# Last gated layer's output product in seven block products on half tiles, with weight sums made in the convolution layer and kept in DRAM

## The reference: what is computed

```python
def mixer_a(h, w_in, b_in, vn_g, vn_b, w_s, b_s, w_out):
    z = gelu(h @ w_in + b_in)                 # (S, 6144)
    u, v = split(z, 2)                        # (S, 3072) each
    v = layernorm(v, vn_g, vn_b)              # then cut into chunks of 128 positions, 8 groups
    gate = einsum('gts,csgd->ctgd', tril(w_s), v) + b_s
    return (u * gate) @ w_out                 # (S, 3072) @ (3072, 1024)
...
def mixer_c(h, w_in, w_dw, b_dw, ln_g, ln_b, w_out):
    a, g = split(h @ w_in, 2)                 # (S, 1024) each
    y = a * sigmoid(g)
    y = causal_depthwise_conv31(y, w_dw) + b_dw
    return silu(layernorm(y, ln_g, ln_b)) @ w_out
...
def channel_mlp(h, w1, w2):
    return square(relu(h @ w1)) @ w2          # 1024 -> 4096 -> 1024
```

## Time and profile before

| | us |
|---|---|
| three runs | 3079.35, 3292.37, 3439.02 (median 3292.37) |
| the profiled execution, its own time | 3079.77 |
| its span on the slowest core (core 3) | 3078.2 |
| around the span | 1.6 |
| spans of the 8 cores | 3070.2 to 3078.2 |

### The profile page before, as it was taken

The page is one execution under the profiler, slowest core; times in us unless marked ns, Lnnn a source line. Parts: engine busy times, 40 slices in busy tenths (PEclk is TensorE's granted clock), DMA queues, the critical chain, the costliest instruction groups (busy, mean ns, idle before and its releaser), DMA issues.

```text
span 3078.2 us, 47408 instructions; the slowest of 8 cores (3070.2 to 3078.2 us)
## 1 busy us (share of the span) xinstructions
PE 3019.1 (98%) x15290; PEld 1439.1 (47%) x15290; DVE 2267.6 (74%) x3775; ACT 1317.5 (43%) x2293; POOL 738.5 (24%) x896
## 2 busy tenths in 40 slices
PE   8999999999999999999999999999999999999998
PEld 3444444444444444444576444444444444444444
DVE  7945767678779987877458788877855757577886
ACT  4312433434655354455534634553322333433554
POOL 1111233101414320132551421212212141201221
PEclk9999999999999999999999999999999999999999
DMA  9699997777867367686422477768897988776674
GB/s 167 109 152 165 165 160 126 164 158 156 165 154 130 62 154 158 150 204 150 104 47 77 100 174 172 166 149 165 140 162 131 160 135 143 155 163 142 153 188 114
DMA packets 137585, 445.45 MB, mean 145 GB/s; under 512 B 12032, under 2 KB 15232, under 8 KB 137344
## 3 DMA queue, kind: packets, MB, share of 16 engines
q0 software_dynamic: 102304, 347.38, 64.4%
q1 hardware_dynamic: 35040, 95.04, 8.7%
HBM read 646.07 MB, written 78.64 MB: 235 GB/s over the span
## 4 chain that ended last, share of the span: by engine, by line
PE 93%; DMA 2%; DVE 2%; issue 1%; ACT 1%; POOL 0%; SPq 0%; DVEq 0%; ACTq 0%; POOLq 0%
PE bank L164 93%; DVE xT L164 1%; DMA xT<-x 1%; DMA x_spill<-xT 1%; DMA ring<-b_w_out 0%; DMA ring<-m_w 0%; DVE m_tv L164 0%; DVE bank L164 0%; DVE hT1v L164 0%; DMA ring<-a_w_in 0%; ACT ring L164 0%; ACT sq L164 0%; ACT rs L164 0%; POOL sacc L164 0%; POOL a_smv L164 0%
## 5 line engine op out<-in xcount | busy, mean ns | idle before, releaser
L164 DVE TENSOR_TENSOR xT<-bank,xT 128x512 f32<-128x512 f32 (+2 forms) x972 | 707.3, 745 | 290.5 <-PE bank L164 270.6
L164 PE MATMUL bank<-m_tv,ring 128*128 128x512 bf16 (+2 forms) x3724 | 814.7, 372 | 11.2 <-DVE xT L164 9.3
L164 PEld LDWEIGHTS bank<-m_tv,ring 128*128 128x128 bf16 x3724 | 358.4, 98 | 434.3 <-issue 24.8
L164 ACT ACTIVATE bank<-bank 128x512 f32<-128x512 f32 x496 | 289.4, 587 | 416.1 <-PE bank L164 340.1
L164 POOL DMA_DIRECT2D ring<-m_w x256 | 137.6, 537 | 1242.4 <-PE bank L164 1189.8
L164 ACT ACTIVATE m_tv<-bank 128x512 bf16<-128x512 f32 x511 | 302.2, 598 | 46.7 <-DVE bank L164 11.2
L164 DVE TENSOR_TENSOR m_tv<-m_tv,m_tv 128x512 bf16<-128x512 bf16 x494 | 221.5, 479 | 97.7 <-ACT m_tv L164 94.9
L164 POOL TENSOR_TENSOR sacc<-sacc,sq 128x512 f32<-128x512 f32 (+1 forms) x162 | 212.0, 1309 | 95.4 <-ACT sq L164 64.0
L164 DVE TENSOR_TENSOR ring<-ring 128x512 bf16<-128x512 bf16 (+1 forms) x384 | 199.9, 537 | 26.7 <-DMA ring<-m_w 18.4
L164 ACT ACTIVATE sq<-xT 128x512 f32<-128x512 f32 (+1 forms) x252 | 152.8, 620 | 144.1 <-POOL sacc L164 91.3
L164 PE MATMUL bank<-m_hv,ring 128*128 128x512 bf16 x704 | 174.6, 379 | 2.2 <-issue 0.3
(11 more groups left out here) (242 smaller groups left out, 4186.5 us busy)
## 6 DMA issues: line engine op xcount, KB each, us to landing
ring<-a_w_in POOLq DMA_DIRECT2D x88, 1024.0 KB, 15.2
ring<-m_w POOLq DMA_DIRECT2D x132, 512.0 KB, 7.1
m_pre<-ring SPq DMA_DIRECT2D x124, 512.0 KB, 6.3
ring<-m_pre POOLq DMA_DIRECT2D x124, 512.0 KB, 7.3
ring<-a_w_out POOLq DMA_DIRECT2D x64, 768.0 KB, 8.5
ring<-m_w POOLq DMA_DIRECT2D x124, 384.0 KB, 6.4
xT<-x SPq DMA_DIRECT2D x16, 512.0 KB, 12.8
ring<-b_w_in POOLq DMA_DIRECT2D x8, 1024.0 KB, 18.7
```

The costliest lines, as they stand in the source:

```text
L164: return lambda e: getattr(e, _method)(*[_r(a) for a in args], **{k: _r(v) for k, v in kwargs.items()})
```

## The change

The output product of layer 3's mixer A (`WO`) is replaced by `WO7`, and only there (`self.seven`); layer 0 keeps `WO`.

- A tile's 512 positions are cut in two halves of 256, the 1024 outputs in two halves, and the 3072 inner channels, in three groups of 8 blocks (`b`), each in two halves of 4 blocks. For each of 4 output pairs `d` there are seven products, each of 3 x 4 = 12 matmuls of 256 columns.
- The sums of activations (`usums`, four DVE operations of 1024 elements for each of the three groups) are made as soon as a group's 8 blocks are through `SP`; three of the four results lie in `v`, the fourth replaces a part of `uT`.
- The sums of weights are made once, in the convolution layer: 12 units, each a load of 2048 elements (1 MB of f32), three DVE operations (`wsums`) and a store of 3584 bf16 elements for each partition to `a_wp` in DRAM, in rows of 512 elements. They use two ring slots lent for that (`lend_slot`, `lent`), so that layer 2 has three, and four from its fourth stage on.
- Each product's weights are then one piece of 128 x 1536 bf16 in DRAM, loaded by SP, two pieces to a slot, 28 pieces for each tile.
- DVE adds a product of 256 columns to `xT` 6 times for each `d`, and one of 512 (a result that goes to two places).
- The norm of the next tile becomes steps within `WO7`; the first V load of tiles 1 to 3 is cut into two halves.

```diff
+    def lend_slot():
+        lent.append(take_slot() + (sc.dma_key(f"unit{len(lent)}"), sc.dma_key(f"unit_out{len(lent)}")))
+
+    def next_unit(after):
+        if makes:
+            d, b = makes.pop(0)
+            lent.append(lent.pop(0))
+            t, r, _, key, out_key = lent[-1]
+            v, vr = views(t, r)
+            sc.op("pool", I("dma_start", out=t[:, 0:2048], in_=dram["a_w_out7"][d * 3 + b], max_dma_last_dim=8192), wr=[vr[k] for k in QUADS[:4]],
+                  cost=0.75, dma=key, nbytes=512 * 2048, after=after, tag="unit", lat=LOAD_LAT)
+            wsums(t, v, vr)
+            sc.op("sp", I("dma_start", out=a_wp[d, :, :, b * 512:(b + 1) * 512].rearrange("k p c -> p k c"),
+                          in_=t[:, 512:4096].rearrange("p (k c) -> p k c", k=7)), rd=[vr[k] for k in QUADS[1:]], wr=[wp_r[d][b]],
...
+            def usums(b):
...
+                for o, x, y in (("S1", "A21", "A22"), ("m2", "A11", "S1"), ("m3", "A21", "A11"), ("n4", "A12", "m2")):
+                    comb(A[(o, b)][0], A[(o, b)][1], *A[(x, b)], *A[(y, b)], ALU.subtract, 1024)
+
+            def WO7(tt, steps):
...
+                def piece(d, wk):
+                    j = place[1] % 2
+                    place[1] += 1
+                    if j == 0:
+                        t, r, key = take_slot()
+                        place[0] = t, r.split(2), key
+                    t, rs, key = place[0]
+                    o = sc.op("sp", I("dma_start", out=t[:, j * 1536:(j + 1) * 1536], in_=a_wp[d, QUADS.index(wk) - 1]),
+                              rd=wp_r[d], wr=[rs[j]], cost=0.06, dma=pc_key[slot_of(t)][j], nbytes=256 * 1536, tag="load")
...
+                for d in range(4):
+                    a, f, e, g = Bank(), Bank(), Bank(), Bank()
+                    prod(a, "A11", "W11", True)
+                    add(a, 0, 0)
+                    prod(f, "A12", "W21", True)
+                    add(f, 0, 0)
+                    prod(e, "m3", "n3", True)
+                    add(e, 1, 1)
+                    prod(a, "m2", "n2", False)
+                    add(a, 0, 1)
+                    prod(g, "n4", "W22", True)
+                    add(g, 1, 0)
+                    prod(e, "A22", "T4", False)
+                    add(e, 0, 1)
+                    prod(a, "S1", "T1", False)
+                    add(a, 1, 2)
+                    if d == 2:
+                        for q in steps:
+                            run_all(q)
...
+            UNIT_AT = (2, 6, 10, 14), (2, 6, 10), (2,), (2, 10), ()
...
+                if i == 3 and lent:
+                    lent.pop(0)
...
                     for vp in range(6):
-                        V(tt, vp, load_v(vp))
+                        V(tt, vp, load_v(vp, 2 if self.seven and tt and vp == 0 else 1))
```

More of the change, by code:

```diff
@@ L549, in take_slot @@
     def take_slot():
-        i = ring_n[0] % NSLOT
-        ring_n[0] += 1
-        return ring[i]
+        while True:
+            i = ring_n[0] % NSLOT
+            ring_n[0] += 1
+            if ring[i][0] not in [x[0] for x in lent]:
+                return ring[i]
     def load_w(name, idx, blk, view, after=(), parts=1):
@@ L1315, in body @@
                     load_x(2, (3,), after=last_sp)
-                    mid = lambda after: self.norm(2, after=after, mode="dve")
+                    mid = lambda after: run_all(self.norm_steps(2, after=after, mode="dve"))
                 elif tt + 1 < NT:
-                    self.norm(tt + 1, after=[late_u[0]])
+                    steps = [self.norm_steps(tt + 1, after=[late_u[0]])]
                 else:
-                    for e in early:
-                        run_all(e)
-                WO(tt, mid)
+                    steps = early
+                if self.seven:
+                    WO7(tt, steps)
+                else:
+                    for q in steps:
+                        run_all(q)
+                    WO(tt, mid)
     class MixB:
@@ L1840, in body @@
             for b in norm_bufs:
[L1841 removed]
+                b.r |= lent_r.used()
+            assert not makes
+            lent.clear()
     for j in range(16):
```

103 lines of the change are left out of this document (76 added, 27 removed).

## The result

The changed kernel takes 3090.6 us (median of 12 executions), the kernel before 3079.5 (12, on the same chip): ratio 1.0033, 95% interval 1.0023 to 1.0043. The time lies inside the range of the forecast, on the other side of the kernel before.

The account below looks back on a forecast made before the run. PE was taken to bound the kernel, 93% of the chain. The terms -17.1 + 4 + 3 + 2 + 3 + 1 = -4.1 on 3079.8 us gave 3075.7, stated as 3076 us, range 3060 to 3100.

Parts of the forecast that it names:

- The products' term: Layer 3's output product: 1344 matmuls of 256 columns for 768 of 512 gain 17.1 us, bounds 13 and 21.
- The rival that it doesn't halve: Layer 3's product: a 256-column matmul does not halve; at 125 ns nothing is gained, 3093 us; chance 0.03.
- that of weight loads that don't overlap: Layer 3's product: 576 more weight loads of 98 ns add 56 us, giving 3132 us; chance 0.02.
- I count no steady wait: Pieces in layer 3's product: loading lags 2.2 us a tile, less than 10 us of supply ahead, so no cost.
- The +4 for the start: Start of each layer 3 product: PE waits for pieces or activation sums, 1 us a tile, +4, from 0 to 12.
- The second rival: Layer 3's product: the SP queue, waiting for slots in turn, starves PE of pieces; 3100 us, slower; chance 0.2.
- V's late start: V of tiles 1 to 3: its first load just arrives, 1 us of wait each, +3, from 0 to 15.
- DVE full in tile 3: Tile 3's product: DVE busy 36.4 of 37.5 us, its delays reach PE through the banks; +2, from 0 to 6.
- The convolution layer and the next MLP: Making weight sums costs the convolution layer +3 (-3 to +12); loads delayed by lent slots and unit stores +1 (0 to 4).
- The stats chain: Convolution layer's stats chain: the last two units' sums before `c_z` cost +3, load and store waits +1.
- the nothing for ten units: Convolution layer stages: ten of twelve units cost nothing, as DVE and DMA have room.
- The third rival: Convolution layer: DVE stands before late units; five or more of 12 cost 3 us each, 3088 us; chance 0.13.

Follow-up runs that it names:

- half pieces: The changed kernel, but each piece's load brings only its first 768 of 1536 columns, with the same 1344 matmuls; ratio 1.0024 to the kernel before.
- whole products: The changed kernel, but from the second column block on a product's 12 matmuls stand together, not in three groups of 4; ratio 1.0011 to the kernel before.
- The run without sums: Layer 3's product as in the kernel before, the twelve units loaded and stored, but DVE's weight sums left out; ratio 1.0026 to the kernel before.
- early norms: On top of whole products, the last MLP's squares allowed from V of tile 2 (tile 0) and in V of tile 3 (tile 1); 3076.1 us, ratio 0.9989.
- the product alone: The changed kernel, but pieces read from the MLPs' stored sums (other weights) and no units made in the convolution layer; ratio 1.0023 to the kernel before.
- the two repairs: Two runs on the changed kernel: whole products, ratio 1.0011 to the kernel before, and early norms on top of it, ratio 0.9989.
- the units alone: All twelve units made and stored in the convolution layer, but layer 3's product left as in the kernel before; ratio 1.0020 to the kernel before.

## Why the prediction was wrong

**The products' term was right.** In the run with half pieces tile 3's product, which has all of its 336 matmuls in its own stage, takes 37.3 us where nothing waits, against 41.7 before: 4.4 a tile, 17.6 in all, for 17.1 forecast. A matmul of 256 columns follows at 109 ns (four in 0.44 us), below the 112 that I took. The rival that it doesn't halve is out, and so is that of weight loads that don't overlap: 1344 of them run beside these matmuls, against the row-group rule of the Trainium skill (TensorE: Matmul & The Clock Gate; the rule stands in its section "The mechanism", not in the one that I named). The 145 to 155 us busy hold too: the profile lists the matmuls as two groups of 100 and 79 us on core 3, but these lie partly over each other, and merged they are busy 151 us.

**"I count no steady wait" failed, and this is the largest part of the miss.** I compared the queue's rate with PE's use and found them level, which they are. What I left out is when the queue may run. I counted 8 pieces ahead as cover from the start; but the matmuls of ten pieces alternate in the product's first 13 us, only one slot comes back in tile 2 (two in the others, by 10 us), and the engines stand still for most of them (the tenths of 0 above). The cover is used up while next to nothing is loaded, and the wait comes 20 us in. The +4 for the start showed nothing but 0.5 us, outside tile 2. In its place there are 0 to 2.3 us a tile in the middle, and up to 5.6 at the end of tile 2's, some of the long ones with 1.7 us of half clock. Supply costs 9.5 us in the median, where I had 0 for it. The second rival had the sign and half of the mechanism (slots in lumps), but gave it to the queue's rate.

**V's late start: forecast +3, measured about 1.** The three V stages are 2.8 us longer in sum (42.5 for 41.6 us), but 16 matmuls of the products stand in them, 1.7 us of it. PE's waits for V's first loads, 8 to 9 us into V, are 0 to 1.8 us in sum, 1.0 in the median core. Whole products take the matmuls out of V, not the waits: these are 0.5 to 2.0 there.

**"DVE full in tile 3" failed by its place and its price: forecast +2, and tile 2 alone is 2.7 us above the others even with half pieces, 7.4 with whole products.** I left the last MLP's norms where the earlier trace rows had them, in tile 3, and I read no row of tile 2. In the changed order tile 0's norm is in tile 2's product, with tile 3's: DVE is busy 38 of 41 to 48 us there, and in tile 3 23.9. And I priced a full DVE by its own operations. It was POOL's squares, 22 us in tile 2 before the change and 25 after it, that made sums of 0.68 us take 1.75. The Trainium skill says this (SBUF — State Buffer, "Who interferes with whom"): a DVE operation with two inputs in SBUF contends with a GpSimd operation that reads SBUF, the shared port is an exclusive lock, and the order of issue decides who is held up. The trace agrees: 1.67 us from sum to sum, beside POOL operations of 1.47. I should have asked of each DVE operation that I added what POOL does beside it.

**The convolution layer and the next MLP: forecast +3 and +1, measured +6.2 and +1.1.** Two of its terms held: the later `c_acc` (+1.3 for +1) and the wait for `c_y` behind the moved `c_T` (2.96 us to 0.8, for -2). At the MLP's start the number is near and the cause another: I had a late load, and PE waits 1.9 us for `mh0v`, a norm made by ACT; it counts in the 6.2, and every run with units, with or without sums, has it. The stats chain was too high, +4 forecast, about +1. What failed is the nothing for ten units, and what hangs on it. Two sums of the second unit stand beside POOL's `c_T` and take 4.4 us for 1.2, so that PE waits up to 2.8 us for `c_y` (0 to 2.1 without the sums). And at the end of the stages, 138 to 146 us into the layer, 0.8 us for `c_yT` on every core and 1.1 to 2.0 before a `c_T` matmul on four are new; for the latter the trace names no releaser. The wait for `c_acc` has 3.4 us of half clock behind it on five cores; before, that for `c_y` had 3.4 to 6.8 on four. The run without sums shows that DVE's part is 6.5 us. The third rival is half of the truth, but no unit came late.

**The slowest core.** My sum, -4, was made for one core. The means of the two profiles differ by +2.4, so it was wrong there by 6 (by 9, when the +4.9 over all executions is taken); the other 8 us are spread, which no term had. That the two cores of a pair are tied together is shown: in all 36 pairs of nine executions they end 4.0 us or more apart, while of two cores of different pairs 65 in 216 end less than 4 apart. In the profile the pairs differ by 14.9 us in the mean: 9.1 of it in the tiles of layer 3, where the kernel before had 0.1, and 6.4 ahead of the convolution layer, where both kernels have the same order and the kernel before had 4.1. The part in the tiles goes with late pieces, to 4.5 with whole products and 2.7 with early norms. The whole distance does so only in part: it is 14.4 in the changed kernel, 16.4 with the product alone, 10.8 and 9.6 with the two repairs, but 11.5 with half pieces, where the tiles are even, and 9.7 with units without sums, where there are no pieces. In this trace core 2 has 12.7 us of waits for pieces and core 3 4.2, with 5.9 and 5.5 us as the median landing of a piece. What they share was not tried; the Trainium skill names a candidate (HBM Reference, "Specifications (TRN2)"): two cores have one HBM domain, and a DMA-bound change is to be measured with both running. That page of the Trainium skill gives 358 GB/s to each of two; the queue's 325 when full are near it.

**Open:** why one of a pair loses throughout an execution, ahead of the changed layers too, the 2.5 us between the stages of the units alone and that run's mean, and whether a unit's sums can stand anywhere in that layer without a price.

## What to carry to other kernels

Compare a loader's supply with its use over time, not by rates alone: ask how long the consumer holds the first slots, since that is how long the queue stands still, and let it finish one slot before it opens the next. An order made by a planner moves work that the change doesn't touch into the space that it opens; look for such guests, on DVE and on POOL together. On a time that is the slowest of eight cores, a margin that one core keeps and its partner misses counts as missed: read the waits on the slower core of each pair, not on one core.

## What the runs showed of the hardware

DVE can be kept out for much longer than one operation. In the run without sums POOL waited 6.1 us for a unit's store, then ran its `c_T` operations without a break, and on core 3 DVE's own `c_T`, which takes 0.95 us in most places, was held until they were through; POOL first, then the line of DVE:

```profile
1576.65 0.55 POOL L164 DMA_DIRECT2D ring<-a_w_out  x1 [6.14 <-DMA a_wp<-ring]
1577.21 15.30 POOL L164 TENSOR_TENSOR c_T<-ring,c_mask 128x1536 bf16<-128x1536 bf16 x5
```

```profile
1578.38 14.96 DVE L164 TENSOR_TENSOR c_T<-ring,c_mask 128x1536 bf16<-128x1536 bf16 x1
```

PE waited 5.1 and 2.8 us for the `c_y` that DVE makes behind it, and that core's layer took 235.6 us instead of 224.5. On the other seven cores the same operation took 1.6 to 3.8 us. With POOL's additions of `sacc`, which have 0.2 us between them, DVE comes in after each one. As I read it, a DMA issue that waits on POOL can so cost DVE its turn later, through the work that it dams up; it is one core in one execution, and no run tries it.
